# Setup stage of a streaming encoder step: modulation weights ahead of the input rows, the row turns spread among the units, the columns one unit later

## The reference, cut to what matters

```python
def ada_norm(x, c, w, b, g):
    m = jax.nn.silu(c) @ w + b                     # c: 9 rows of 1024; w: 1024 x 3072, one per sub-layer
    shift, scale, gate = jnp.split(m[:, None, :], 3, axis=-1)
    return rmsnorm(x, g) * (1 + scale) + shift, gate
```

## Time and profile before

| | us |
|---|---|
| median of three runs | 4101.99 (4099.0 to 4108.2) |
| the profiled execution, its own time | 4112.55 |
| its span | 4111.0 |
| TensorE busy / VectorE busy / ScalarE busy | 3575.6 / 2129.3 / 1365.0 |
| end of the setup block, start of attention | 209.7 |

### The profile page before, as it was taken

How to read it: one execution, slowest core, us unless ns; L and a number is a source line. 1 busy time by engine, 2 the same in 40 slices (tenths; PEclk the granted TensorE clock), 3 DMA queues, 4 the chain that set the end, 5 groups by cost and what they waited for, 6 DMA issues and landing times. The chain is left out here.

```text
span 4111.0 us, 53886 instructions
## 1 busy us (share of the span) xinstructions
PE 3575.6 (87%) x20685; PEld 2102.0 (51%) x20917; DVE 2129.3 (52%) x3527; ACT 1365.0 (33%) x2660; POOL 479.5 (12%) x1002
## 2 busy tenths in 40 slices
PE   6867888777697999999978888888888899999996
PEld 3535455544353555555534555555554455555553
DVE  4644444445445555555545554555544655555553
ACT  5534444344323122222124444444432222122122
POOL 0002122223110000000000222211200000000000
PEclk9888887778798999999989999999998999999998
DMA  7721122112311111111121333333331011111111
GB/s 290 276 59 59 58 83 75 54 47 62 102 35 45 38 47 41 37 47 42 40 66 38 115 115 110 115 105 111 106 114 55 29 47 42 37 47 41 37 37 47
DMA packets 222722, 303.33 MB, mean 74 GB/s; under 512 B 24848, under 2 KB 174969, under 8 KB 221910
## 3 DMA queue, kind: packets, MB, share of 16 engines
q1 hardware_dynamic: 193046, 190.24, 13.9%
q0 software_dynamic: 29504, 110.77, 8.4%
HBM read 264.23 MB, written 63.95 MB: 80 GB/s over the span
## 5 line engine op out<-in xcount | busy, mean ns | idle before, releaser
L96 PE MATMUL psum<-h,ffn_high 128*128 128x512 f32 (+1 forms) x2112 | 1035.9, 531 | 48.2 <-DVE hl L474 48.2
L98 PE MATMUL psum<-hl,ffn_high 128*128 128x512 bf16 (+1 forms) x2028 | 616.6, 337 | 0.0
L100 PE MATMUL psum<-h,ffn_low 128*128 128x512 bf16 (+1 forms) x2066 | 578.9, 332 | 2.9
L96 PE MATMUL psum<-actr,ffn_high 128*128 128x512 f32 (+1 forms) x1056 | 517.2, 530 | 15.7 <-DVE actl L807 15.7
L96 PEld LDWEIGHTS psum<-h,ffn_high 128*128 128x128 f32 x2112 | 409.4, 194 | 135.3 <-issue 43.9
L98 PEld LDWEIGHTS psum<-hl,ffn_high 128*128 128x128 bf16 x2112 | 206.3, 98 | 431.7 <-issue 372.8
L86 PE MATMUL psum<-h,attC_high 128*128 128x384 f32 x744 | 367.5, 494 | 40.2 <-DVE hl L474 23.2
L86 PE MATMUL psum<-h,attAB_high 128*128 128x384 f32 x648 | 333.6, 515 | 39.0 <-DVE hl L474 23.4
L784 DVE TENSOR_SCALAR y<-u,cvT 128x1168 f32<-128x1168 f32 x88 | 78.2, 888 | 530.0 <-ACT u L735 530.0
L98 PE MATMUL psum<-actl,ffn_high 128*128 128x512 bf16 (+1 forms) x1012 | 308.0, 337 | 0.0
L100 PE MATMUL psum<-actr,ffn_low 128*128 128x512 bf16 (+1 forms) x1034 | 290.3, 332 | 1.5
(11 more groups left out here) (441 smaller groups left out, 7129.6 us busy)
## 6 DMA issues: line engine op xcount, KB each, us to landing
ada_raw<-in_ada_w SPq DMA_DIRECT2D x48, 1024.0 KB, 7.7
ffn_raw<-in_w_up SPq DMA_DIRECT2D x88, 512.0 KB, 3.6
ffn_raw<-in_w_down SPq DMA_DIRECT2D x44, 512.0 KB, 3.7
raw_C<-in_cache_c_k POOLq DMA_DIRECT2D x64, 256.0 KB, 3.4
raw_C<-in_cache_c_v POOLq DMA_DIRECT2D x64, 256.0 KB, 3.0
out_ck_s<-in_cache_c_k POOLq DMA_DIRECT2D x8, 1984.0 KB, 8.7
out_cv_s<-in_cache_c_v POOLq DMA_DIRECT2D x8, 1984.0 KB, 14.3
attC_raw<-in_w_in_odd SPq DMA_DIRECT2D x24, 512.0 KB, 4.7
```

The source lines that it names most:

```text
L96: return pe.matmul(out, w, x[:, lo:hi], start=first and start, stop=last and stop, skip_group_check=True)
L98: return pe.matmul(out, top(w), xl[:, lo:hi], start=first and start, stop=last and stop, skip_group_check=True)
L100: return pe.matmul(out, wl, top(x[:, lo:hi]), start=first and start, stop=last and stop, skip_group_check=True)
```

## The change: what it does, and the diff

SP's list becomes: the rows of c, the constants, chunks 0 to 5, the input rows, chunks 6 to 47. The 16 small loads go to POOL's list, behind its memsets. TensorE starts the units at once; two turns stand behind the chunks of each of units 1 to 9, and their copies on ACT stand among the splits of the next unit. The exponential on ACT, the two `lam` products and the small vectors on DVE stand inside units 0 to 2. The columns of modulation a-1 stand behind the first unit of modulation a, and their removal by DVE behind the second split of the unit after it. The last modulation's columns stay at the end. The core of the diff:

```diff
+    units = [(a, j) for a in range(4) for j in range(3)]
+    turns = [range(max(0, 2 * u - 2), min(18, 2 * u)) for u in range(len(units))]
...
     def _(sp):
-        sp.dma_start(K[:, :], ins["consts"][:, 0:C_L]).then_inc(S.const_in, 16)
...
         sp.dma_start(crow[0:1, :], ins["c_prompt"]).then_inc(S.c_in, 16)
         sp.dma_start(crow[1:NC9, :], ins["c_sample"]).then_inc(S.c_in, 16)
...
+        sp.dma_start(K[:, :], ins["consts"][:, 0:C_L]).then_inc(S.const_in, 16)
+        for c in range(6):
+            chunk(c)
         for t in range(0, QB, 2):
             sp.dma_start(xrow[:, t:t + 2, :], ...).then_inc(S.x_in[t // 2], 16)
         sp.dma_start(xrow[:, QB, :], ...).then_inc(S.x_in[QB // 2], 16)
-        for a in range(4):
-            for j in range(3):
-                for c in range(KT // 2):
-                    ring.load(sp, ada_chunk(a, j, c), ada_w[a, j, c], ...)
+        for c in range(6, FBASE):
+            chunk(c)
...
     def _(pool):
+        (the memsets of cst and cb first, then ada_b, norm_g, final_g, subln_g, conv_w, conv_b,
+         mask rows, lam_*, rel_bias, sinks: the loads that left SP's list)
...
     def _(act):
+        for u, (a, j) in enumerate(units):
+            for k in range(KT // 2):
+                c = ada_chunk(a, j, k)
+                if c + 3 < FBASE:
+                    ring.split_high(act, c + 3)
+                if u and k % 2 == 0 and k // 2 < len(turns[u - 1]):
+                    x_evac(act, turns[u - 1][k // 2])
+            if u == 1:
+                act.wait_ge(S.lam_dot, 2)
+                act.activation(lams[:, 2:4], lams[:, 0:2], ACT.Exp).then_inc(S.lam_exp, 1)
+            last = ada_chunk(a, j, KT // 2 - 1)
+            act.wait_ge(S.f_used[last % 3], last // 3 + 1)
+            if a and j == 0:
+                act.wait_ge(S.mod_mm, a)
+            act.copy(msb[0:2 * NC9, j * D:(j + 1) * D], ...).then_inc(S.ada_evac, 1)
...
     def _(pe):
+        for u, (a, j) in enumerate(units):
+            (the 32 matmuls of unit u, as before)
+            for q in turns[u]:
+                turn(q)
+            if u == 1:
+                (wait for the small vectors, transpose them)
+            if a and j == 0:
+                columns(a - 1)
+        columns(3)
...
     def _(dve):
+        for u, (a, j) in enumerate(units):
+            for k in range(KT // 2):
+                c = ada_chunk(a, j, k)
+                if c + 3 < FBASE:
+                    ring.split_low(dve, c + 3)
+                if a and j == 1 and k == 1:
+                    modulation(a - 1)
+            if u == 0:
+                lambdas()
+            elif u == 2:
+                vectors()
+        modulation(3)
```

More of the change, by code:

```diff
@@ L273, in _ @@
     def _(pool):
+        pool.memset(cst[:, :, :].bitcast(F32), 0.0).then_inc(S.set_zero, 1)
+        pool.memset(cb[:, :, :], 0.0).then_inc(S.set_zero, 1)
         pool.memset(G.ones[:, :], 1.0).then_inc(S.set_ones, 1)
         pool.memset(G.eps[:, :], EPS).then_inc(S.set_ones, 1)
[L276 to L277 removed]
         pool.memset(rev[:, 0:P], 0.0).then_inc(S.rev_made, 1)
@@ L297, in _ @@
             ring.split_high(act, c)
[L298 to L315, removed]
+        for u, (a, j) in enumerate(units):
[12 more added lines that the diff above has]
+                act.wait_ge(S.mod_mm, a)
+            act.copy(msb[0:2 * NC9, j * D:(j + 1) * D],
+                     ps[0:2 * NC9, 2 * (u % 2):2 * (u % 2) + 2, :].rearrange("p b n -> p (b n)")).then_inc(S.ada_evac, 1)
     @block.tensor
     def _(pe):
-        pe.wait_ge(S.const_in, 32)
+        pe.wait_ge(S.const_in, 16)
         pe.wait_ge(S.csil, 1)
@@ L323, in _, with turn @@
         mm.then_inc(S.small_ready, 1)
[L324 to L330, removed]
+        pe.wait_ge(S.c_low, 2)
+        def turn(q):
             t, half = q // 2, q % 2
@@ L336, in _, with columns @@
                 kk = 4 * half + k
-                mm = pe.transpose(ps[:, 6 - 2 * (q % 2), k * P:(k + 1) * P], xrow[:, t, kk * P:(kk + 1) * P], ident)
+                mm = pe.transpose(x_bank(q)[:, k * P:(k + 1) * P], xrow[:, t, kk * P:(kk + 1) * P], ident)
             mm.then_inc(S.x_turned, 1)
[L339 to L355, removed]
+        def columns(a):
             pe.wait_ge(S.ada_evac, 3 * (a + 1))
             pe.wait_ge(S.adab_in, 16 * (a + 1))
-            if a:
-                pe.wait_ge(S.mod_evac, a)
+            pe.wait_ge(*((S.mod_evac, a) if a else (S.small_evac, 1)))
             for n in range(24):
@@ L388, in _ @@
         dve.tensor_copy(cb[:, :, 0:NC9], cst[:, :, 0:NC9].bitcast(F32)).then_inc(S.c_low, 1)
[L390 to L403, removed]
-        ch.then(dve.tensor_copy(gT[:, :], ps[:, 7, 0:41]))
@@ L405, in _ @@
-        ch.then(dve.tensor_copy(cvT[:, :, :, :].rearrange("p l j t -> p (l j t)"), ps[:, 7, 64:416]))
-        dve.tensor_scalar(G.gsub[:, :], gT[:, 40:41], 1.0 - LAM_INIT, None, ALU.mult).then_inc(S.small_evac, 1)
-        for a in range(4):
-            for j in range(3):
-                for k in range(KT // 2):
-                    c = ada_chunk(a, j, k)
-                    if c + 3 < FBASE:
-                        ring.split_low(dve, c + 3)
+        for c in range(3):
+            ring.split_low(dve, c)
@@ new lines, in lambdas @@
+        def lambdas():
+            dve.wait_ge(S.lam_in, 64)
+            for j in range(2):
+                dve.tensor_tensor_reduce(out=lamp[:, j, :], in0=lamv[:, 2 * j, :], in1=lamv[:, 2 * j + 1, :], scale=1.0,
+                                         scalar=0.0, op0=ALU.mult, op1=ALU.add,
+                                         accum_out=lams[:, j:j + 1]).then_inc(S.lam_dot, 1)
+            dve.wait_ge(S.tab_in, 16)
+            dve.tensor_scalar(rev[:, P:384], tab[:, 255::-1], tab[:, 256:257], 1.0 / SCALE, ALU.subtract,
+                              ALU.mult).then_inc(S.rev_made, 1)
@@ L413, in _, with modulation @@
+        def modulation(a):
             dve.wait_ge(S.mod_mm, a + 1)
```

97 lines of the change are left out of this document (64 added, 33 removed).

## The result

The changed kernel takes 4077.89 us (median of 5 runs, 4072.22 to 4085.17) against 4103.47 for the kernel before in the same comparison (5 runs): ratio 0.9943, 95% interval 0.993 to 0.9957. The gain is 25.6 us, forecast 23.3; the time forecast was 4079. Run again later (6 runs) it took 4083.15 against 4104.08, ratio 0.9938 (0.9921 to 0.9955). So the gain is 21 to 26 us.

What follows compares the result with a forecast made beforehand. Transfers bound the kernel up to 47.1 us, then DVE inside a modulation, with everything standing between modulations. The setup's end moves from 209.7 to 186.4, and 4101.99 - 23.3 gives 4078.7 us; range 4069 to 4092.

Steps and rivals of the forecast that it cites:

- 1, first chunk: Head of the setup: chunk 0, issued at about 2.0, lands at 8.5 us, 1.5 charged for small loads' packets.
- 2, the rows come back: Behind chunk 5: 4.5 MB of input rows delay chunk 6, done at 39.0; 21.1 of 36 us are left.
- 3, to the first columns: Chunk 6 to 15: transfers set the pace, 22.5 us, plus vectors 2.7 and lower clock 1.0; chunk 15 at 65.2.
- 4, a hole: Between modulations: `msb` wait goes, columns take 8.3, ACT and DVE run dry; chunk 19's low part begins at 82.8.
- 5, two periods: Two modulation periods: 39.75 us each, from 41.9, turns and removal together adding 1.4; chunk 43's low part at 162.3.
- 6, tail: End of the setup: five low parts 11.5, one removal 0.65, then 11.9 as before; setup ends at 186.4.
- 7, covered: SP's bias table, the exponential, `lam` products and POOL's loads stay hidden; the table ends near 168, 18 us of cover.
- the main term: Lead at chunk 6 in the setup: done at 39.0 instead of 60.2, so 21.1 us are left.
- long columns, heavy turns: Rival, setup: columns take 10.1 three times (+5.4), turns delay the ring (+3); gain 15, 4087 us; chance 0.27.
- free small work: Rival, setup: small packets, vectors and cold start cost nothing, columns take 7.7; gain 30, 4072 us; chance 0.13.
- at the lower clock through the units: Rival, TensorE at 1.2 GHz: a chunk takes 3.9, a unit 6.4 more; 4137 us if throughout units 1 to 9; chance 0.04.
- The bubble closes: Rival, between modulations: three ready chunks hide the columns, three holes of about 12 go; near 4045 us; chance 0.01.

Runs made afterwards that it cites:

- the second profile: The changed kernel run once more, unaltered, against the kernel before: 4083.15 us (6 runs) against 4104.08, ratio 0.9938; setup end 182.55.
- the head alone: The changed kernel with the columns back behind their own modulation's third unit, against the kernel before: 4090.10 us against 4101.58, ratio 0.9972.
- the first kernel with spread columns: The changed kernel with columns cut into pieces among the next unit's chunks, in one PSUM bank: 4079.57 us, ratio 0.9945 to the kernel before.
- the last two kernels: Changed kernel with columns spread in two banks and input rows spread: 4053.69 us, ratio 0.9883; same with first pieces later and evenly cut: 4055.57, ratio 0.9884.

## Why the prediction was right, step by step

- *1, first chunk.* Forecast to land at 8.5, split at 7.49: right within 1 us, with no delay by small packets in it yet.
- *2, the rows come back.* Right in kind: the hole opened between chunks 5 and 6. Off in size: from chunk 0 to chunk 6 it took 30.3 us, not 10.5 x 2.50 = 26.3, because the small loads beside the first chunks cost about 4.0 us and not the 1.5 that I charged (my bound was 3.5). Chunk 6 was done at 42.00, forecast 39.0. This was the term most mis-sized in the head; the experiment with the small loads on SyncE's list shows the first chunks at full pace without them.
- *3, to the first columns.* From chunk 6 to chunk 15 26.0 us, forecast 26.2. Its parts: the splits of chunks 6 and 15 are 23.9 apart (37.78 and 61.68), 22.5 of it transfers, which at 420 GB/s set most of the pace. The 1.4 above it is ScalarE, forecast 1.0: it waited 1.33 us for TensorE at chunk 9, and had work without a pause from 50.18 on, among it a table load of 1.28 for the exponential, which ran behind chunk 10's split and not in the hole where I had put it. The vectors on VectorE end at 65.76, directly before chunk 15's low part, and account for the other 2.1 (2.7).
- *4, a hole.* 67.97 to 84.51 is 16.5, forecast 17.6. To the release 2.0 (2.3), two turns 1.04 (1.2), columns 7.74 (8.3), one chunk at the granted clock of 0.50 3.90 (3.9). The lead is 17.7 (19.4).
- *5, two periods.* 38.63 and 35.72, forecast 39.75 each: the largest error, 5.2 us in all. 2.6 of it is the columns (8.25 and 5.75, not 8.3 twice), whose length depends on where the clock falls. The other 2.6 is turns and removal inside the units, for which I charged 1.4 a period: without columns the periods took 30.4 and 30.0. The kernel before has 29.0 (41.70 - 9.75 - 2.95); with the turns' 1.04 ahead of the columns that is 30.0, which leaves 0.4 and 0. The other turns and the removal were hidden.
- *6, tail.* Five low parts and the removal 12.5, forecast 12.2. From the last low part's end (171.37) 13.1, forecast 11.9: the last columns took 8.91, not 7.66.
- *7, covered.* SyncE's third store was issued at 166.54 and landed 3.1 us later, near 169.6 (forecast 168), 15 us before the end: right.

The sum: +3.0, -0.2, -1.1, -5.2, +0.3 and +1.2 give -1.9 us, 184.5 for 186.4. The forecast is close because errors of 3 and 5 us cancelled; the mechanism holds step by step, the precision of the total is luck.

Three of the signs that I had named need an answer. Chunk 6 did come late because small loads held the weights back, by 3.0 us: its split at 37.78 lies between the 35 that I had called right and the 42 that I had called wrong. VectorE was idle 8 to 10 us at the columns, not 11 to 13. And the stretch behind the setup was 12.8 us shorter, which I had called a sign of being wrong; the second profile shows that it is scatter.

One sentence of mine was wrong in weight: I called the 21.1 us of lead at chunk 6 "the main term". The experiments give the head alone 11.5 us and the later columns alone 14 to 17. The lead at chunk 6 was 18.2 (60.2 - 42.0). With the columns in the old place 13.7 of it were left when TensorE came to wait ahead of them (74.15 and 60.44, the columns' starts less the waits), and 10.5 at their start (77.09 - 66.61): the wait for the small vectors, 3.2 us longer, takes the difference. The other 4.5 go between chunk 6 and that wait, 1.0 of them on the two turns that now stand there.

Of the rivals, *long columns, heavy turns* did not come (columns 7.7, 8.3, 5.8, turns hidden), nor *free small work* (the packets cost more). TensorE *at the lower clock through the units* did not either: 0.97 from 82.6 to 109.0. The Trainium skill's section "A second HAM failure mode: psum-queue depth-cycling" (TensorE: Matmul & The Clock Gate) describes a kernel in which frequent short idle times between groups of matmuls made the clock go up and down; the turns and hand-overs of the changed kernel did not bring that about. In the first kernel with spread columns, where TensorE waited up to 3.18 us for its bank, the clock from 74 to 85 us was 0.73; in the last two kernels, with waits of up to 0.9 us for the columns and 1.7 us for chunks, it was 1.00 from 30 us to the end of the chunks. Whether that rule is at work there I can't say. *The bubble closes* was right for a kernel that wasn't this one: I had argued that three ready chunks can't hide a block of columns, and when the block was cut into pieces that they can, the kernel gained another 24 to 29 us, rows spread included.

## What to carry to other kernels

A serial piece of work on the consumer of a ring stops every producer once it is longer than the ring's depth hides: here 6 to 8 us of columns, with the slower chunk behind them, left VectorE idle for 8 to 10. Moving it as a block to another place took off its wait and some of its length. Cutting it into pieces hid it, provided that the pieces didn't wait for a single output buffer; part of that gain was the clock. Loading the needed data first wins little if the rest of the queue takes it back later: give bulk data that is needed late its place between the urgent loads, at the rate at which it is used. Moving small loads from one engine's list to another's can trade slower transfers for later issues, and the profile tells them apart: a full busy share at fewer GB/s is the one, a low share the other. And when the unchanged rest of a kernel varies by up to 17 us from profile to profile, read a change of 25 from the end of its stage and from repeated runs.

## What the runs showed of the hardware that I had not expected

- The same 24 small matmuls (48 records) took 5.63 to 10.41 us within this study, by where the granted clock fell: 5.75 in a stretch at 0.95, 7.74 at 0.69, 8.91 at 0.59, 9.75 at 0.54. Which it is changes between two runs of the same kernel, and with it the setup's end (182.55 and 184.50; 187.14 and 192.41).
- Sixteen small loads (vectors in short rows, and broadcasts to 128 partitions) beside six chunks of 1 MB cost the 16 DMA engines about 4 us. The share of busy engines does not tell: it is 1.02 at 314 GB/s with them and 1.03 at 421 GB/s without. On the list that also issues the chunks they cost as much, but by a queue that ran nearly empty: 216 GB/s at a share of 0.65 from 30 to 36 us.
- The weight chunk behind a block of columns ran at a granted clock of 0.50 in all three cases of the changed kernel's profile, 3.90 us in place of about 2.0, even behind the columns of 5.75 us, during which the clock was at 0.95. With columns in two banks and rows spread the clock was 1.00 from 60 to 152 us, and this cost was gone too.
